# Gate and up of two SwiGLU layers in 16 groups of seven block products, three passes a layer

## What is computed

```python
def swiglu(h, w_gate, w_up, w_down):
    return (jax.nn.silu(h @ w_gate) * (h @ w_up)) @ w_down

for l in range(DEPTH):                     # DEPTH = 2
    ...
    x = x + swiglu(rms_norm(x, ffn_norm[l]), w_gate[l], w_up[l], w_down[l])
return rms_norm(x, final_norm)
```

## Time and profile before

| | us |
|---|---|
| median of three runs | 1771.25 |
| span of the profiled execution, first to last instruction | 1769.1 |
| TensorE matmuls busy | 1761.5 (100%) |
| VectorE busy | 1130.7 (64%) |
| ScalarE busy | 914.3 (52%) |
| GpSimd busy | 113.1 (6%) |
| DMA traffic | 328.79 MB, 186 GB/s on average |

### The profile page before, as it was taken

How to read it: one execution, slowest core, us unless ns; L and a number is a source line. 1 busy time by engine, 2 the same in 40 slices (tenths; PEclk the granted TensorE clock), 3 DMA queues, 4 the chain that set the end, 5 groups by cost and what they waited for, 6 DMA issues and landing times.

```text
span 1769.1 us, 29325 instructions
## 1 busy us (share of the span) xinstructions
PE 1761.5 (100%) x10438; PEld 1564.0 (88%) x10438; DVE 1130.7 (64%) x1460; ACT 914.3 (52%) x1176; POOL 113.1 (6%) x132
## 2 busy tenths in 40 slices
PE   9999999999999999999999999999999999999998
PEld 6888888888888888889999888888888888888887
DVE  5766666556666666678997776666655566666554
ACT  6666664334444453456775466666533344445433
POOL 2100000000000001124111420000000000000000
PEclk9999999999999999999999999999999999999999
DMA  7555556545555566545445555555665455556642
GB/s 282 195 188 190 189 197 229 191 155 177 190 190 190 190 223 196 175 152 160 148 137 179 190 184 191 189 188 188 230 200 166 162 190 190 190 190 222 227 146 72
DMA packets 86017, 328.79 MB, mean 186 GB/s; under 512 B 9680, under 2 KB 11088, under 8 KB 85840
## 3 DMA queue, kind: packets, MB, share of 16 engines
q1 hardware_dynamic: 85680, 327.03, 55.5%
q10 hardware_dynamic: 288, 1.11, 0.2%
HBM read 326.01 MB, written 2.10 MB: 185 GB/s over the span
## 4 chain that ended last, share of the span: by engine, by line
PE 100%; DVE 0%; issue 0%; DVEq 0%; ACT 0%; POOL 0%; POOLq 0%
PE ps L435 58%; PE ps L436 31%; PE ps L505 2%; PE ps L443 1%; PE ps L445 1%; PE ps L444 1%; PE ps L799 1%; PE ps L798 1%; PE ps L797 1%; PE ps L633 0%; PE ps L632 0%; PE ps L631 0%; PE ps L685 0%; PE ps L493 0%; PE ps L705 0%; PE ps L706 0%
## 5 line engine op out<-in xcount | busy, mean ns | idle before, releaser
L1238 DVE TENSOR_TENSOR w_lo<-raw,w_hi 128x1024 fp32r<-128x1024 f32 (+2 forms) x564 | 736.0, 1308 | 419.1 <-ACT w_hi L850 416.9
L435 PE MATMUL ps<-xg,w_hi 128*128 128x512 f32 x2880 | 999.7, 390 | 0.0
L850 ACT ACTIVATE w_hi<-raw 128x1024 fp32r<-128x1024 f32 (+2 forms) x565 | 630.9, 1120 | 548.9 <-PE ps L436 533.2
L436 PE MATMUL ps<-xg,w_lo 128*128 128x256 f32 x2880 | 812.1, 282 | 0.0
L435 PEld LDWEIGHTS ps<-xg,w_hi 128*128 128x128 f32 x2880 | 540.5, 188 | 113.5 <-DVE w_lo L1238 0.3
L436 PEld LDWEIGHTS ps<-xg,w_lo 128*128 128x128 f32 x2880 | 544.3, 189 | 0.1
L435 PE MATMUL ps<-act,w_hi 128*128 128x512 f32 x1320 | 458.0, 390 | 0.0
L436 PE MATMUL ps<-act,w_lo 128*128 128x256 f32 x1320 | 372.2, 282 | 0.0
L435 PEld LDWEIGHTS ps<-act,w_hi 128*128 128x128 f32 x1320 | 247.7, 188 | 51.9
L436 PEld LDWEIGHTS ps<-act,w_lo 128*128 128x128 f32 x1320 | 249.5, 189 | 0.0
L1318 DVE TENSOR_TENSOR sums<-ps,cross 128x512 f32<-128x512 f32 x88 | 60.8, 691 | 93.1 <-ACT cross L928 93.1
(11 more groups left out here) (200 smaller groups left out, 1240.2 us busy)
## 6 DMA issues: line engine op xcount, KB each, us to landing
raw<-w_gate SPq DMA_DIRECT2D x176, 512.0 KB, 3.2
raw<-w_up SPq DMA_DIRECT2D x176, 512.0 KB, 3.2
raw<-w_down SPq DMA_DIRECT2D x120, 704.0 KB, 4.2
raw<-w_o SPq DMA_DIRECT2D x32, 512.0 KB, 3.2
raw<-w_last SPq DMA_DIRECT2D x11, 512.0 KB, 3.2
raw<-w_q_a SPq DMA_DIRECT2D x8, 512.0 KB, 3.2
raw<-w_kv_a SPq DMA_DIRECT2D x8, 512.0 KB, 3.3
raw<-w_q_nope SPq DMA_DIRECT2D x8, 512.0 KB, 3.2
```

The source lines that it names most:

```text
L435: pe.matmul(ps[:, bank, :], w_hi[:, s, j * P:(j + 1) * P], moving, start=start, stop=False)
L436: return pe.matmul(ps[:, bank, 0:SEQ], w_lo[:, s, j * P:(j + 1) * P], moving[:, 0:SEQ], start=False, stop=stop)
L850: nc.scalar.activation(dst, src, ACT.Copy).then_inc(hi_ready, 1)
L1238: nc.vector.tensor_tensor(lo, src, hi.bitcast(F32), ALU.subtract).then_inc(lo_ready, 1)
```

## The change

**Seven products for eight.** A *group* is two hidden tiles. Its gate and up together are one product of x (256 tokens by 2048 features) and a matrix of 2048 features by 512 columns. Both are cut in two along features, x also along tokens and the weights along the two hidden tiles (gate and up of one tile side by side, 256 columns): weight quarters W11, W12, W22, W21, each of two chunks. Strassen's scheme takes seven products of 128 tokens x 1024 features x 256 columns in place of eight. Here the activations are the stationary operand and the weights move, 256 columns at a time, with three matmuls for each block (`group_chunk`). A group is 14 chunks of 12 matmuls; 16 groups stand in for 32 of the 88 hidden tiles.

**Sums of weights.** Three of the seven products use quarters as loaded, the other four use sums. `add_quarter` on VectorE forms them in place in `raw`, each in two chunks of 1024 elements a partition: W12 is added to W11 after P1's split, W22 after P5's, W22 to W12 after P6's, and W11 to W21 after P2's. That is eight sums a group, beside 14 splits.

**Sums of activations.** Four mixed blocks of x (`mix_hi_lo`) are formed once a layer, in the first 14 chunks of its first pass (`mix_step`): four `corner` products of x and gain, four sums and four low parts on VectorE, four high parts on ScalarE. The corners and sums lie in raw slots 4 to 7, those of W22 and W21. The loads of these quarters wait for the last mixed block.

**Results.** Group results are token-major in PSUM (the chain of banks 4 and 5 and bank 6). ScalarE copies three partial sums out and applies Silu four times (`part_copy`, `part_gate`), VectorE adds three times and multiplies four times (`part_sum`, `part_times`), TensorE transposes four blocks (`turn_parts`), and both engines split the result (`group_act`). The token factor is needed by rows too, from two more small matmuls a layer.

**Order.** A layer has three passes, of 16, 14 and 14 hidden tiles with 2, 3 and 3 groups. In a pass plain chunks lead (20 or 4), then group chunks are mixed with 21 plain ones (three plain to four group chunks in the first pass, one plain to two in the others), and 7 plain chunks close it. `raw` has 8 slots for quarters and down chunks, and 3 for plain gate and up chunks. The up part is written out without loops.

The core of the diff:

```diff
-FH = D_FF // P // 2
+PASSES = 6
+PASS_TILES = (16, 14, 14, 16, 14, 14)
+PASS_GROUPS = (2, 3, 3, 2, 3, 3)
+PASS_LEAD = (20, 4, 4, 20, 4, 4)
+PASS_TAIL = 7
+MIX_STEPS = 14
-WEIGHT_SLOTS = 8
+RING_SLOTS = 8
+PLAIN_SLOTS = 3
...
+PRODUCTS = ("P1", "P5", "P6", "P2", "P7", "P3", "P4")
+QUARTERS = ("W11", "W12", "W22", "W21")
+READS = {"P1": "W11", "P5": "W11", "P6": "W11", "P2": "W21", "P7": "W12", "P3": "W22", "P4": "W21"}
+def up_loads(q):
...
+            before = PLAIN_NO[n] - PLAIN_SLOTS
+            free = PLAIN_AT[before] if before >= 0 else 0
+            loads.append((max(free, CHUNK[UPS[q]] - 1), n, ("chunk", n)))
...
+                if free == 0 and q % LAYER_PASSES == 0 and w in ("W22", "W21"):
+                    free = CHUNK[UPS[q]] + MIX_STEPS
...
+    return [load for _, _, load in sorted(loads, key=lambda x: x[:2])]
...
+            def load_quarter(q, g, w, c):
...
+                    if q % LAYER_PASSES == 0 and w in ("W22", "W21"):
+                        sp.wait_ge(mix_ready, 4 * (q // LAYER_PASSES + 1))
+                row = (g * len(QUARTERS) + QUARTERS.index(w)) * 2 + c
+                sp.dma_start(raw[:, s, :], w_group[row]).then_inc(landed[s], 16)
...
+            def group_chunk(q, k):
...
+                    wh, wl = (w[:, s, j * WIDE:(j + 1) * WIDE] for w in (w_hi, w_lo))
+                    pe.matmul(dst, x_hi, wh, start=(kt == 0 and r in ("P1", "P5")), stop=False,
+                              skip_group_check=True)
+                    pe.matmul(dst, x_hi, wl, start=False, stop=False, skip_group_check=True)
+                    mm = pe.matmul(dst, x_lo, wh, start=False, stop=(kt == TILES - 1),
+                                   skip_group_check=True)
+                mm.then_inc(chunks_used, 1)
+            def turn_parts(g):
...
+                for k, at in enumerate((0, 3, 1, 2)):
+                    mm = pe.transpose(ps[:, STATS, k * P:(k + 1) * P], part[:, at, P:], const[:, C_IDENT:C_IDENT + P])
...
+            def add_quarter(g, into, w, c, done):
+
+                src, dst = quarter_slot(w, c), quarter_slot(into, c)
+                ve.wait_ge(landed[src], 16 * LOAD_NO["quarter", g, w, c])
+                nc.vector.tensor_tensor(raw[:, dst, :], raw[:, dst, :], raw[:, src, :], ALU.add).then_inc(done, 1)
+
+            def split_up(n):
+
+                split(n)
...
+                if step[2] == "P1":
+                    add_quarter(g, "W11", "W12", step[3], first_sum)
+                elif step[2] == "P5":
+                    add_quarter(g, "W11", "W22", step[3], second_sum)
+                elif step[2] == "P6":
+                    add_quarter(g, "W12", "W22", step[3], third_sum[step[3]])
+                elif step[2] == "P2":
+                    add_quarter(g, "W21", "W11", step[3], fourth_sum[step[3]])
...
+            def mix_step(q, k):
+
+                if k == 4:
+                    ve.wait_ge(chunks_used, CHUNK["up0"])
+                    corner(q, 4, 0, 0)
+                elif k == 5:
+                    corner(q, 6, 0, 1)
+                elif k == 6:
+                    corner(q, 7, TILES, 1)
+                elif k == 7:
+                    mix_sum(q, 0, 7, 7, 6, ALU.subtract)
+                elif k == 8:
+                    mix_sum(q, 1, 6, 4, 6, ALU.subtract)
+                elif k == 9:
+                    mix_sum(q, 2, 4, 4, 7, ALU.add)
+                    mix_low(q, 0)
+                elif k == 10:
+                    corner(q, 5, TILES, 0)
+                    mix_low(q, 1)
+                elif k == 11:
+                    mix_sum(q, 3, 5, 4, 5, ALU.subtract)
+                    mix_low(q, 2)
+                elif k == MIX_STEPS - 1:
+                    mix_low(q, 3)
...
+                for k in range(len(UP_ORDER[q])):
+                    if stats is not None and k == 3:
+                        rstd_of(stats)
+                        row_rstd_of(q // LAYER_PASSES)
+                    if q % LAYER_PASSES == 0 and k < MIX_STEPS:
+                        mix_step(q, k)
...
+                    split_up(CHUNK[UPS[q]] + k + SPLIT_SLOTS)
```

More of the change, by code:

```diff
@@ new lines, with load_numbers @@
+UP_LOADS = [up_loads(q) for q in range(PASSES)]
+def load_numbers():
+    numbers, count, order = {}, [0] * (RING_SLOTS + PLAIN_SLOTS), []
+    for n in range(CHUNK["end"]):
+        q = up_pass(n)
+        if q is None:
+            order.append(("chunk", n))
+        elif n == CHUNK[UPS[q]]:
+            order += UP_LOADS[q]
+    for load in order:
+        s = raw_slot(load[1]) if load[0] == "chunk" else quarter_slot(*load[2:])
+        count[s] += 1
+        numbers[load] = count[s]
+    return numbers
@@ L117 @@
+LOAD_NO = load_numbers()
 SQUARED = (DT, DT, LT, LT - 2, DT)
@@ L330, in trunk, with ended, tile_ended, times @@
         INIT = 3
-        UPS = ("up0", "up1", "up2", "up3")
-        DOWNS = ("down0", "down1", "down2", "down3")
+        def ended(q, k, product):
+            order = UP_ORDER[q]
+            if 0 <= k < len(order) and order[k][0] == "S" and order[k][2:] == (product, 1):
+                return GROUPS_BEFORE[q] + order[k][1]
+            return None
+        def tile_ended(q, k):
+            order = UP_ORDER[q]
+            if 0 <= k < len(order) and order[k][0] == "P" and order[k][2] == 3:
+                return order[k][1]
+            return None
+        def times(q, k):
+            last = len(UP_ORDER[q]) - 1
+            return range(k, k + 1) if k < last else range(last, last + 3)
+        def done_at(q, k):
+            return CHUNK[UPS[q]] + k + 1
         @block.sync
@@ L375, in _, with ffn @@
             sp.dma_start(pos_i[:, :], positions.partition_broadcast(P)).then_inc(pos_landed, 16)
[L377 to L401, removed]
+            def ffn(q):
+                for kind, *which in UP_LOADS[q]:
+                    if kind == "chunk":
+                        load_plain(*which)
+                    else:
+                        load_quarter(q, *which)
+                layer, k = divmod(q, LAYER_PASSES)
+                w, first = (w_down_first, layer * 2 * DT) if k == 0 else (
+                    w_down_rest, (layer * (LAYER_PASSES - 1) + k - 1) * 2 * DT)
+                tiles = LAST_DT if q == PASSES - 1 else DT
+                for c in range(BODY):
+                    load(CHUNK[DOWNS[q]] + c, w[first + c])
+                with sp.Fori(0, tiles // 4 - 1) as i:
+                    for c in range(BODY, 2 * BODY):
+                        load(CHUNK[DOWNS[q]] + c, w[plus(first + c, i, BODY)], i)
+            for q in range(LAYER_PASSES):
+                ffn(q)
             for c in range(2 * LT):
@@ L549, in _, with plain_chunk @@
             mix(2)
[L551 to L554, removed]
+            def plain_chunk(q, k):
+                _, p, c = UP_ORDER[q][k]
+                n, t, half = CHUNK[UPS[q]] + k, TILE[UPS[q]] + 2 * p + c // 2, c % 2
+                pe.wait_ge(lo_ready, made(n))
                 if half == 0:
-                    peel = 1
-                    if layer == 0:
+                    bank_free(t)
+                for j in range(TILES):
+                    kt = half * TILES + j
+                    mm = product3(n, j, t % 4, xg[:, kt, :], kt == 0, kt == DT - 1)
+                mm.then_inc(chunks_used, 1)
@@ L964, in down @@
                     split(n1 + 2 * d + SPLIT_SLOTS, i)
-                    if half == 1 and layer == 0:
+                    if q == LAYER_PASSES - 1:
                         gained(d, t1 + d + 1, G_ATTN, xg, i, 4)
```

576 lines of the change are left out of this document (446 added, 130 removed).

## The result

The changed kernel takes 1790.32 us (median of three runs, 1790.17 to 1791.6) against 1771.25; the ratio is 1.0109, 95% interval 1.0095 to 1.0122. The forecast was 1782.5 in 1757 to 1806.

A forecast was written before the change was run, and what follows sets the result against it. TensorE, busy for the whole span at 2.4 GHz, was taken as the bound. 1769.1 - 23.0 + 0.7 + 12 + 8.8 + 10.2 + 2.6 = 1780.4 us of span, so 1782.5 us median, range 1757 to 1806.

The forecast's parts named there:

- term 1: TensorE, gate and up: seven products for eight save 1.44 us a group, -23.0 us for 16 groups.
- 2 row factors: TensorE: two more small float32 matmuls a layer, 0.34 us, twice: +0.7 us.
- 3 three passes: Seams of the added passes: down matmuls stay as many and the seams are covered, nothing; at most 1 us each.
- 4 dense groups: 14-tile passes: weight sums make VectorE late near the plain chunk after P6b, +12 us; bounds 0 and 33.
- 5 mixing: Mixing x, steps 4 to 11: VectorE needs 26.8 us against TensorE's 22.2, +8.8 for both layers; bounds 4 and 11.
- 6 held loads: Chunk 18 of up0 and up3: its load stands behind W22 and W21, +10.2 us for both layers; bounds 1 and 16.
- 6 first group afterwards: After the chunk 18 wait, the first group's sums meet a VectorE without a lead: 1.3 us a layer, +2.6.
- the disputed matmul: TensorE's 256 column group matmul, priced at 0.1183 us; 0.1155 from below, 0.119 from above.
- the sentence on what is covered: ScalarE, the DMAs and written-out code in place of loops were taken as covered, costing nothing.
- A: VectorE is covered: the lead of four slots takes up the weight sums, 1750 us; chance 0.17.
- B: The four quarter loads ahead of chunk 18 hold nobody up: 1770 us, no change; chance 0.15.
- C: Every VectorE operation costs its whole length, 1.23 us: 1806 us; chance 0.18.

The follow-up runs named there:

- e4_nosum: Changed kernel with the sums of weight quarters left out (one-element adds, wrong weights), TensorE's work unchanged: 1771.3 us, 19 less.
- e3_angles: Changed kernel with the 13 rotary angle operations moved from the beginning of up1 to two output tiles before the end of down0: 1785.0 us, 5.3 less.
- e2_spread: Changed kernel with mixing spread to one VectorE operation a step (MIX_STEPS 17 for 14, which also moves the W22 and W21 loads): 1769.8 us, 20.5 less.
- e8_all: Changed kernel with later W22 and W21 loads, spread mixing, moved angles and reordered plain chunks together: 1752.55 us, ratio 0.9894 to the kernel before.
- e1_order: Changed kernel with the first group's W22 and W21 loads queued behind those of plain chunks 18, 19 and 22: 1775.5 us, 14.8 less.
- e5_level: Changed kernel, 14-tile passes reordered: six plain chunks among P1 to P2, one among P7, P3, P4: 1791.9 us, 1.6 more.
- e7_level2: Changed kernel, 14-tile passes reordered: six plain chunks among P1 to P2, the seventh between a group's last chunk and the next P1: 1777.1 us, 13 less.

## Why the prediction was right, point by point

The forecast had the sign, and the places and the order of three of the four losses; the measured slowdown is 19.1 us where it said 11.3. In part the closeness is luck: term 1 was too small by 5.4 us, which hid as much of what was missed on the other side.

| term | forecast | measured | from |
|---|---|---|---|
| 1 seven products for eight | -23.0 | -28.4 | 1.77 us a group in e4_nosum |
| 2 row factors | +0.7 | +0.9 | 0.43 us in layer 0, twice |
| 3 three passes | 0 | 0 | down stages |
| 4 dense groups | +12 | +16.3 | 4 x 4.07, e4_nosum |
| 5 mixing | +8.8 | +7.1 | three waits a layer |
| 6 held loads | +10.2 | +10.6 | wait before chunk 18, twice |
| 6 first group afterwards | +2.6 | 0 (no wait over 0.3 us) | TensorE's timeline of up0 |
| the angles | not seen | +5.3 | e3_angles |
| lower clock | not seen | +5.8 | windows |

The measured terms make 17.6 of 19.2 us of span; the 0.5 us before up0 and waits under 0.3 us are most of the rest. The waits of terms 5 and 6 are counted by distance, from one matmul's start to the next less the usual 0.12 us, which is 0.16 us more than the idle time in the row. The last row and the wait before chunk 18 share 1.7 us: without the first stretch at the lower clock the held loads would have cost 12.3 us in place of 10.6, and the lower clock 4.1 in place of 5.8.

**Term 1** was mis-sized in the transposes, not in the disputed matmul. The row of eight instructions for 0.87 us is eight transposes, not four; a group's four take 0.36 us:

```profile
163.46 0.60 PE L817 MATMUL ps<-const,part 128*128 128x128 f32 x4
163.82 0.37 PE L802 MATMUL ps<-w_hi,xg 128*128 128x256 f32 x1
```

The groups' matmuls stand 0.1184 us apart where nothing is waited for (mean of 2539 distances in the kernel after), beside the 0.1183 taken from the earlier trace rows. The formula of the Trainium skill ("TensorE: Matmul & The Clock Gate", "Back-to-back issue gap"), which that section gives for an isolated matmul, makes 109 ns, and that is not reached here either. From its parts a group would gain 22.18 - 168 x 0.1184 - 0.36 = 1.9 us; why the stages show 1.77 is open.

**Term 4** had the mechanism, the second and third group and the chunk: the three waits of up4 end at 1381.5, 1426.4 and 1429.0 us, before the plain chunk after P6b and beside it, and last 0.9, 0.6 and 0.9 us. The sums cost a third more than forecast, 4.07 us a pass for 3. The waits alone are 2.4 us a pass; the other 1.7 are in shorter ones and in slower matmuls behind each wait, of which e4_nosum has none.

**Terms 5 and 6** came out within 2 us each, by the count in the table. Term 5 was too large by 1.7; of that the six low parts make 0.4, as each costs VectorE 1.14 us from start to start (85.57 to 86.71 in the rows of the worst step) where the forecast took 1.2. The bound from below of term 6 (0.5 us a layer, were VectorE on time) was never tested, since e2_spread also moves the loads. The 1.3 us a layer for the first group did not come in the kernel after, but 2.1 us did in e2_spread.

**What failed** is the sentence on what is covered: it looked at ScalarE, the DMAs and the code, but not at VectorE's work between the passes, which the diff leaves in place. The angles were hidden by 88 chunks in a row in the kernel before and are not behind a lead of four. It put the angles at nothing, and they cost 5.3 us. And the sum took waits as plain time, where TensorE can pay again in the clock.

**Rivals.** A (VectorE covered, 1750 us) is close to what e8_all reached, 1752.55, where the same operations and loads only stand in other places; as the kernel stands it is false. B is false by e1_order. C is false by VectorE's rows in up4, where nothing is waited for:

```profile
1417.76 1.21 DVE L1592 TENSOR_TENSOR w_lo<-raw,w_hi 128x1024 fp32r<-128x1024 f32 x1
1418.90 1.21 DVE L1672 TENSOR_TENSOR raw<-raw 128x1024 f32<-128x1024 f32 x1
1420.03 1.21 DVE L1592 TENSOR_TENSOR w_lo<-raw,w_hi 128x1024 fp32r<-128x1024 f32 x1
```

The starts are 1.14 and 1.13 us apart with sums in place and signals on each. The Trainium skill's rule ("VectorE: DVE Perf Modes", "The DRAIN you can't avoid") that the next operation does not start until the pipeline is empty does not describe these rows, whose durations (1.21) overlap. The same section adds that an operation that is not held starts earlier, and with that the rows agree.

## What to carry to other kernels

A saving on a full engine is kept only where each helper stays ahead of it chunk by chunk: add up the helper's work and the lead for the worst stretch, not for the cycle, and the average of 98% here says little, since the same work in another order gained 3 us a pass. Before blaming a full helper, try to move its work apart, look for loads queued behind a wait for it, and list what else already stands in its program at the places whose cover the change takes away. An order change can itself make a new wait, as e5_level did; its trace tells that from "order does not help". And when one constant of a kernel sets two things, as `MIX_STEPS` does, an experiment that changes it tests both at once.

## What the runs showed of the hardware

The three early waits of 0.8, 0.5 and 1.8 us stand in up0 and up3 of six kernels (the one after and all the others but e2_spread and e8_all). In six of these twelve places a stretch of 3.4 us at the lower clock follows within 1.5 us of the last of them (in up0 of the kernel after, from 90.5 us), in the other six none does (among them up3 of the kernel after and up0 of e3_angles, e4_nosum and e7_level2). So the same waits in the same work can be followed by a fall or not. Each of the ten waits before chunk 18, of 3.6 to 6.7 us, met the lower clock, before its end or within 1.2 us after it, for 3.4 or 6.8 us. At the lower level a pair takes 0.64 us against 0.35. In e8_all, whose longest wait is 0.6 us, the clock stays at its upper level until the last stage's end. What a wait must be to be followed by a fall was not tried.

The first matmul after a wait is longer in the rows: 0.50 us for 512 columns at 89.31, against 0.39. The 0.79 us at 104.41 were taken at the lower clock, where such a matmul shows 0.63.
